# Rotary halves of the queries in a fused decoder step: one fp32 exchange of sine products, or two fp32r exchanges of a rounded part and its rest

## The reference, cut to what matters

```python
def rope(x, pos):
    ang = pos[:, None] * inv[None, :]
    cos, sin = jnp.cos(ang), jnp.sin(ang)
    x1, x2 = jnp.split(x.astype(jnp.float32), 2, axis=-1)
    return jnp.concatenate([x1 * cos - x2 * sin, x2 * cos + x1 * sin], axis=-1)

def mla_query(hn, w_dq, q_norm, w_uq, w_uk, pos):
    cq = rmsnorm(hn @ w_dq, q_norm)
    q = (cq @ w_uq).reshape(B, L, N_HEADS, QK_NOPE_DIM + QK_ROPE_DIM)
    q_nope, q_rope = q[..., :QK_NOPE_DIM], q[..., QK_NOPE_DIM:]
    q_rope = rope(q_rope, pos)
```

## Time and profile before

| | us |
|---|---|
| median of 3 runs | 736.03 |
| lowest, highest | 735.76, 736.8 |
| profiled execution, its own time | 736.79 |
| its span, first to last instruction | 735.1 |
| TensorE busy in it | 725.5 |
| query stage, first query product to first keys | 370.1 to 400.8 |

### The profile page before, as it was taken

One profiled execution on the slowest core, in us unless ns is written; L12 is line 12 of the kernel. 1 busy time (PEld: TensorE's weight loads), 2 busy tenths in 40 slices (PEclk: granted clock), 3 DMA queues, 4 the chain that ended last, 5 costly groups with the idle time before them and its releaser, 6 DMA issues.

```text
span 735.1 us, 16687 instructions
## 1 busy us (share of the span) xinstructions
PE 725.5 (99%) x6255; PEld 709.1 (96%) x6255; DVE 306.8 (42%) x777; ACT 408.4 (56%) x743; POOL 534.9 (73%) x252
## 2 busy tenths in 40 slices
PE   9999999999999999999999999999999999999995
PEld 8999999999999999999999888799999999999995
DVE  5446986233333222232488766753233333221002
ACT  7877555455444444555677576665554444444542
POOL 4895778869878888889868122149878878888891
PEclk9999999999999999999999999999999999999999
DMA  7864455656777755566576898326546555556641
GB/s 260 260 207 139 134 169 176 201 173 211 241 238 231 235 186 173 199 200 203 174 255 192 263 386 310 134 68 218 174 148 198 183 186 180 191 171 197 203 146 60
DMA packets 44842, 144.68 MB, mean 197 GB/s; under 512 B 5650, under 2 KB 6674, under 8 KB 44530
## 3 DMA queue, kind: packets, MB, share of 16 engines
q1 hardware_dynamic: 44498, 143.50, 59.3%
q0 software_dynamic: 144, 0.40, 0.1%
q10 hardware_dynamic: 144, 0.02, 0.0%
HBM read 142.42 MB, written 1.48 MB: 196 GB/s over the span
## 4 chain that ended last, share of the span: by engine, by line
PE 95%; DVE 2%; ACT 1%; DMA 1%; issue 0%; SPq 0%; DVEq 0%; ACTq 0%
PE ps L1373 29%; PE ps L1374 29%; PE ps L1375 29%; PE ps L1774 1%; PE ps L1750 1%; PE ps L1694 1%; DMA h<-xT 1%; PE ps L1503 1%; PE ps L1621 0%; PE ps L1754 0%; PE ps L1412 0%; PE ps L1680 0%; ACT whi L480 0%; DVE ps L851 0%; PE ps L1682 0%
## 5 line engine op out<-in xcount | busy, mean ns | idle before, releaser
L414 POOL TENSOR_TENSOR wlo<-raw,whi 128x1024 fp32r<-128x1024 f32 x221 | 527.1, 2409 | 182.5 <-ACT whi L480 182.4
L1373 PE MATMUL ps<-xhi,whi 128*128 128x264 f32 x1000 | 286.9, 287 | 0.0
L1374 PE MATMUL ps<-xlo,whi 128*128 128x264 f32 x1000 | 283.3, 283 | 0.0
L1375 PE MATMUL ps<-xhi,wlo 128*128 128x264 f32 x1000 | 283.2, 283 | 0.0
L480 ACT ACTIVATE whi<-raw 128x1024 fp32r<-128x1024 f32 x221 | 232.7, 1054 | 50.5 <-PE ps L1375 48.3
L1374 PEld LDWEIGHTS ps<-xlo,whi 128*128 128x128 f32 x1000 | 188.5, 189 | 0.2
L1373 PEld LDWEIGHTS ps<-xhi,whi 128*128 128x128 f32 x1000 | 188.3, 188 | 0.3
L1375 PEld LDWEIGHTS ps<-xhi,wlo 128*128 128x128 f32 x1000 | 187.6, 188 | 0.0
L1373 PE MATMUL ps<-ahi,whi 128*128 128x264 f32 x352 | 100.0, 284 | 0.0
L1375 PE MATMUL ps<-ahi,wlo 128*128 128x264 f32 x352 | 99.9, 284 | 0.0
L1374 PE MATMUL ps<-alo,whi 128*128 128x264 f32 x352 | 99.9, 284 | 0.0
(11 more groups left out here) (266 smaller groups left out, 1148.8 us busy)
## 6 DMA issues: line engine op xcount, KB each, us to landing
raw<-w_stream SPq DMA_DIRECT2D x221, 512.0 KB, 3.4
pg<-pages SPq DMA_DIRECT2D x64, 288.0 KB, 4.5
pg<-w_ukT SPq DMA_DIRECT2D x1, 2048.0 KB, 9.3
pg<-w_uv SPq DMA_DIRECT2D x1, 2048.0 KB, 10.0
h<-xT SPq DMA_DIRECT2D x4, 264.0 KB, 4.7
raw<-w_stream SPq DMA_DIRECT2D x4, 256.0 KB, 5.5
y_out<-raw SPq DMA_DIRECT2D x4, 198.0 KB, 2.3
wsraw<-wsT SPq DMA_DIRECT2D x1, 512.0 KB, 5.6
```

Of the source, the lines that this page charges most:

```text
L414: pool.tensor_tensor(wlo[:, c % RING, :], raw[:, c % RING, :], whi[:, c % RING, :].bitcast(F32), ALU.subtract).then_inc(lo_ready, 1)
L1373: pe.matmul(out, whi_, mhi, start=start, stop=False)
L1374: pe.matmul(out, whi_, mlo, start=False, stop=False)
L1375: return pe.matmul(out, wlo_, mhi, start=False, stop=stop)
```

## The change

The queries' rotary chunk is no longer multiplied by the sine ahead of the exchange. ScalarE makes its rounded part `rhi`, VectorE its rest `rlo`, and TensorE exchanges both with an fp32r copy of the permutation, `swap_r`, as two products into the same bank. VectorE then multiplies the exchanged values by the sine in place and subtracts them from the cosine products. The swap of pair p stands after the first chunk of pair p+1, one pair at a time, and the steps of ScalarE and VectorE on the turned queries are written pair by pair too. GpSimd makes `swap_r` with four small copies, early in the kernel. The swap of the keys' rotary part is as before.

```diff
+        swap_r = sb("swap_r", [P, P], F32R)
+        rhi, rlo = xhi[:, 4:6, :], xlo[:, 4:6, :]
...
+            for z in range(4):
+                pool.tensor_copy(swap_r[:, 32 * z:32 * z + 32],
+                                 ident[:, 32 * (z ^ 1):32 * (z ^ 1) + 32]).then_inc(swap_done, 1)
...
             def queries(p, done):
 
+                wait_query(act, 3 * p)
+                if p > 1:
+                    act.wait_ge(rope_swap, p - 1)
+                act.activation(rhi[:, p % 2, :], ps[:, 0, 0:T], ACT.Copy).then_inc(rope_hi, 1)
                 for e in range(2):
                     x = 3 * p + 1 + e
+                    if e and p > 1:
+                        turned_queries(p - 1)
                     wait_query(act, x)
...
-            for g in range(1, PAIRS // 2):
-                turned_queries(2 * g - 2)
-                turned_queries(2 * g - 1)
-                done = queries(2 * g, done)
-                if g == 2:
+            turned_queries(0)
+            for p in range(2, PAIRS):
+                done = queries(p, done)
+                if p == 4:
                     act.wait_ge(c_done, KL)
                     act.activation(cThi[:], ps[:, 6:8, 0:NP_], ACT.Copy).then_inc(cthi_done, 1)
-                done = queries(2 * g + 1, done)
-                if g == 2:
+                if p == 5:
                     act.activation(cT[:], ps[:, 6:8, 0:T], ACT.Copy).then_inc(ct_done, 1)
...
                 if p > 1:
                     dve.wait_ge(rope_swap, p - 1)
                     dve.wait_ge(qr_done, p - 1)
-                dve.tensor_tensor(tt[:, 1 + p % 2, :], ps[:, 0, 0:T], sinb, ALU.mult).then_inc(rope_sin, 1)
+                dve.wait_ge(rope_hi, p + 1)
                 dve.tensor_tensor(sq[:, p % 2, :], ps[:, 0, 0:T], cosb, ALU.mult).then_inc(rope_cos, 1)
+                lo_of(rlo[:, p % 2, :], ps[:, 0, 0:T], rhi[:, p % 2, :]).then_inc(rope_lo, 1)
...
             def query_turned(p):
 
+                dve.wait_ge(rope_swap, p + 1)
+                dve.tensor_tensor(turned_bank(p), turned_bank(p), sinb, ALU.mult).then_inc(rope_sin, 1)
                 dve.wait_ge(rope_cos, p + 1)
-                dve.wait_ge(rope_swap, p + 1)
-                dve.tensor_tensor(turned_bank(p), turned_bank(p), sq[:, p % 2, :], ALU.add).then_inc(qr_done, 1)
+                dve.wait_ge(rope_sin, p + 1)
+                dve.tensor_tensor(turned_bank(p), sq[:, p % 2, :], turned_bank(p), ALU.subtract).then_inc(qr_done, 1)
...
+            for p in range(2, PAIRS):
+                query_rope(p)
+                query_turned(p - 1)
+                query_low(p, 0)
+                query_turned_low(p - 1)
...
+                if p == 7:
                     latents_low()
-                query_low(2 * g + 1, 1)
...
+                query_low(p, 1)
+            query_turned(PAIRS - 1)
...
                 elif z == 0:
+                    pe.wait_ge(rope_lo, p)
                     pe.wait_ge(rope_cos, p)
...
-                pe.matmul(turned_bank(p), swap, tt[:, 1 + p % 2, :], start=True, stop=True).then_inc(rope_swap, 1)
+                pe.matmul(turned_bank(p), swap_r[:], rhi[:, p % 2, :], start=True, stop=False)
+                pe.matmul(turned_bank(p), swap_r[:], rlo[:, p % 2, :], start=False, stop=True).then_inc(rope_swap, 1)
 
             def queries(p):
                 for z in range(3):
                     query_chunk(p, z)
+                    if p and z == 0:
+                        query_swap(p - 1)
```

More of the change, by code:

```diff
@@ L264, in build @@
             sem, ("gqs_done", "c_done", "ct_done", "cthi_done", "ctlo_done", "zero_done"))
-        q_done, qnhi_done, qlow_done, rope_cos, rope_sin, rope_swap, qr_done, qrhi_done, qrlo_done = map(
-            sem, ("q_done", "qnhi_done", "qlow_done", "rope_cos", "rope_sin", "rope_swap", "qr_done", "qrhi_done", "qrlo_done"))
+        q_done, qnhi_done, qlow_done, rope_cos, rope_hi, rope_lo, rope_swap, rope_sin, qr_done, qrhi_done, qrlo_done = map(
+            sem, ("q_done", "qnhi_done", "qlow_done", "rope_cos", "rope_hi", "rope_lo", "rope_swap", "rope_sin", "qr_done", "qrhi_done", "qrlo_done"))
         qns_done, qrs_done, qsr_done, ql_done, qla_done, qlb_done, qlt_done, qsla_done, qslb_done = map(
@@ L783, in sample_out @@
                 act.activation(os_[:, s, :], ps[:, 7, 0:LAT], ACT.Copy).then_inc(os_done, 1)
-            turned_queries(PAIRS - 2)
             keys_high(0)
@@ L1181, in _ @@
             query_low(1, 0)
+            query_turned(0)
             query_low(1, 1)
[L1183 to L1197, removed]
+            query_turned_low(0)
+            for p in range(2, PAIRS):
[3 more added lines that the diff above has]
+                query_turned_low(p - 1)
+                if p < 4:
+                    latents(p - 2)
+                if p == 5:
                     dve.memset(qsr[ROPE:P, 0], 0.0).then_inc(qsr_done, 1)
                     dve.memset(qsr[0:ROPE, 1], 0.0).then_inc(qsr_done, 1)
-                if g == 3:
+                if p == 7:
                     latents_low()
-                query_low(2 * g + 1, 1)
-            for p in (PAIRS - 2, PAIRS - 1):
-                query_turned(p)
-            query_turned_low(PAIRS - 2)
+                query_low(p, 1)
+            query_turned(PAIRS - 1)
             def keys_low(p):
@@ L1611, in query_swap @@
             def query_swap(p):
-                pe.wait_ge(rope_sin, p + 1)
+                pe.wait_ge(rope_hi, p + 1)
+                pe.wait_ge(rope_lo, p + 1)
+                pe.wait_ge(swap_done, 8)
                 if p == 0:
@@ L1632, in _ @@
             pe.matmul(ps[:, 5, 0:T], swap, Ra, start=True, stop=True).then_inc(krswap_done, 1)
[L1633 to L1636, removed]
+            for p in range(1, PAIRS):
                 queries(p)
-                queries(p + 1)
-            query_swap(PAIRS - 2)
             query_swap(PAIRS - 1)
```

## The result

The changed kernel takes 742.7 us (median of 6 runs, 741.6 to 743.78), the kernel before on the same chip 736.18 us (6 runs). The ratio is 1.0085, with a 95% interval of 1.0075 to 1.0096: slower by 6.3 us, between 5.5 and 7.1 (the two medians lie 6.5 apart). The forecast was 741.0 us, slower, with a range of 739.5 to 743.2. One execution of the later run e8 took 1014.65 us at a mean clock of 0.655; it is left out of every comparison. The profiled execution took 741.6 us, with a span of 739.9 us.

A forecast was written before the change was run, and what follows sets the result against it. TensorE, busy for 725.5 of 735.1 us, was taken as the bound. Pauses of 6.6 us less 1.63 us saved gave 4.96 us more: 741.75 us for the profiled execution, 741.0 us for the median, range 739.5 to 743.2.

The forecast's parts named there:

- the working: Whole kernel: the forecast for the profiled execution, 741.75 us, from one execution of 736.79 us before the change.
- the walk: Query stage: start times of ScalarE's roundings, pair by pair, up to the keys, which come 4.96 us later than before.
- The saving: TensorE, query stage: 16 fp32r products (1.93 us) replace 8 fp32 swaps (3.56 us), saving 1.63 us.
- The ring: Query stage: queues wait on each other, one turn 4.19 us against TensorE's 3.50; 741.0 us, chance 0.85.
- The last pause: TensorE ahead of the keys: waits about 2.4 us for VectorE's rest of the latents; keys at 405.78.
- The clock: Rival, chance 0.07: pauses lower the clock to 1.2 GHz, 3.4 us from the keys on become 6.8; 744.4 us.
- Costed at nothing: GpSimd, early in the kernel: four copies take another 0.62 us, covered by 1.4 us of slack.
- No pauses: Rival, chance 0.04: in the query stage the queues slide past each other, only the 1.63 us saving is left; 734.4 us.
- only the end: Rival, chance 0.04: only the 2.4 us wait ahead of the keys is left, less 1.63 us saved; 736.8 us.

The follow-up runs named there:

- e8: The changed kernel run again with nothing altered, on the same chip: 743.3 us.
- e6: Changed kernel with the latents' rest one pair earlier on VectorE and ScalarE's splits of pairs 2 to 4 behind the first plain chunk: 738.72 us.
- e7: Changed kernel's arithmetic with the steps of ScalarE and VectorE and the swaps' places ordered anew: 735.38 us, ratio 0.9989 to the kernel before.
- e3: Changed kernel with the rest of the latents made by VectorE one pair earlier (pair 6 instead of 7): 740.77 us.
- e4: Changed kernel with 14 idle fp32r products on TensorE ahead of the wait for the keys: 741.93 us.
- e1: Kernel before, its arithmetic and fp32 swap kept, put in the changed kernel's pairwise order: 740.86 us, ratio 1.0057.
- e2: Changed kernel's new products in the order of the kernel before, by groups of two pairs: 741.59 us, ratio 1.0066.

## Why the prediction was right, and where it was too small

Its direction, cause and place were right; its size was 4.96 us where 6.3 were measured. e6 and e7 show the cause: e6 moves three splits and the latents' rest and takes back 3.5 us of the distance, and e7 runs the new products in a third order below the time of the kernel before. Against the forecast of 741.0 us the median is 1.7 higher: 0.7 in the executions in which the clock stays up, whose median is 741.68, and 1.0 by those in which it falls. The profiled execution seems to fit better, 741.6 us where the working gave 741.75, but that is luck: its stage is 1.0 us longer than the walk, and it is short by as much before and behind the stage, as told at the end of this section.

- *The saving.* 16 products at the price of any other, no stretched one behind. It shows in e7, once nothing waits.
- *The ring.* Right in every step, a little too short. I had 4.19 us for a turn; it is 4.38. Rounding to cosine is 384.72 to 385.24, 0.52 instead of 0.42, so the way from ScalarE to VectorE took 0.12 us and not 0.03 (the cosine stands behind four waits in the code, the row that gave 0.03 behind one; no run tests whether that is why). Sine product to subtraction is 0.53 instead of 0.47. These two make 0.16 of the 0.19.
- *The walk.* The changed kernel's execution came to the query stage 0.61 us earlier than the one of before (373.24 and 373.85 for the keys' swap). With that added, the roundings of pairs 2 to 7 stand at 380.95, 385.33, 389.71, 394.56, 398.84 and 402.29, where I had 380.94, 385.27, 389.46, 394.20, 398.04 and 401.28. The largest miss of one turn is pair 5's, 4.28 for 3.84: VectorE's cosine started 0.49 us after the end of the rounding instead of 0.12. That rounding stands right behind the wide one of the latents. It is no accident of one execution, since e3, e4, e6 and e8 have the same 0.49 us there; why it is late is open.
- *The last pause.* From the last rounding to the keys I had 4.50 us, it is 4.53. TensorE idled for 2.11 us, ended by `cTlo`, as said. In all, the keys come 6.00 us later and not 4.96; the turns' 1.0 us is the whole difference.
- *The clock.* I gave this rival 7% as a case for itself, at +3.4 us. By the spans it is true in more than half of the executions (6 of the 10 counted have 741.3 or more; one of the six was profiled and shows the fall), and it costs 1.6 us, since the clock was back before the sample queries were through: at 407.2 in e1, where they end at 408.64. The step that failed in this rival is the length of the slow stretch: it took all the work from the keys to the end of the sample queries as slow, and only 3.4 us by the clock were, some 1.7 us of work. So the two rivals were not either-or: the ring makes the pause, and the pause at times brings the clock down. The Trainium skill (TensorE: Matmul & The Clock Gate, section "HAM oscillation — how this bites in real kernels") tells of a kernel in which the wait for data between bursts of products lets the clock down every time, so that each burst starts slow. Those waits are longer than any pause here, and the runs show that a shorter one can be enough: 3.40 us at a mean of 0.51 behind the pause in e1, with 1.92 us idle, though it does not happen in every execution of the changed kernel.
- *Costed at nothing.* GpSimd's four copies took 0.62 us (37.05 to 37.67), its next rest ended at 41.1, and TensorE took up that slab at 41.82, without a wait.
- *No pauses* and *only the end* fell: e1 and e2 show that the queues do hold each other, in either order.

The distance went up by 6.00 us, the span of the profiled execution by 4.8 only. 0.61 of the rest is that it came to the stage earlier. Another 0.55 us lie behind the last layer's products, between line 1908 (1913 now) and the end of the span: 9.11 us in the profile of before, 8.56 in the changed kernel's, 8.5 to 8.9 in those of e1 to e8. So it is the profile of before that stands out there, and no experiment aimed at it.

## What to carry to other kernels

Before an engine is given a step that another engine's step must wait for, add up one whole turn of the waits, with everything that stands in the queues between them, and compare it with the time that the bound engine needs for the same turn; the loads of the engines alone do not show it (here both were below the 3.50 us of a turn, by the prediction's rows, and the turn took 4.38). An order that was right for one set of dependences must be found anew for another: the same arithmetic was 6.3 us slower than before in one order and 0.9 us faster in another. And when TensorE must pause for a couple of microseconds, fillers in the pause can give back what the clock would take behind it: 1.55 us of the distance in e1, and nothing in an execution in which the clock stays up anyway (36.36 us in e4, 36.32 without fillers).

## What was not expected of the hardware

- A pause of TensorE of about 2 us is enough for the granted clock to go to 1.2 GHz behind it, though not each time: in e1 (1.92 us idle) the profile shows it and the spans of all five executions fit it, in the changed kernel (2.11 us idle) 6 of 10. The longer of the two pauses has the rarer fall, so its length alone does not decide; what does is open. In e2, with three waits of 1.2 to 1.4 us each among full stretches, the profile has the clock at 1.00 throughout the stage, and the five spans lie within 1.0 us. A fall costs 1.5 to 1.6 us.
- Idle products in a pause were no loss: 15 of them made e1 faster by 1.7 us, and 14 left the changed kernel's distance where it was in the execution without a fall.
- Of steps of VectorE on 128 x 264 values, one that waits for nothing came 0.34 us after the one ahead. Steps that work in place in one bank of PSUM, each behind a wait for the one ahead, came 0.47 us apart before the change. The subtraction, which waits for two things (`rope_cos` and `rope_sin`), came 0.53 us behind the sine product. What makes the 0.06 us is not shown. The rows from before:

```profile
374.99 0.43 DVE L861 SCALAR_TENSOR_TENSOR ps<-ps,work 128x264 f32<-128x264 f32 x1
375.46 0.44 DVE L864 SCALAR_TENSOR_TENSOR ps<-ps,work 128x264 f32<-128x264 f32 x1
```
